# Summing modulation products over partitions: the data as the stationary operand, two columns of ones moving

## The reference

```
for l in range(2):
    m  = (silu(c)     @ w_mod[l] + b_mod[l])   # 9 x 1024, w_mod[l] is 1024 x 9216
    mc = (silu(c_ctx) @ w_mod[l] + b_mod[l])   # the same weights, other vector
    x  = ffn_sublayer(x,  m,  0, ...)          # x + 0.5*m[2] * swiglu(norm(x)*g*(1+m[1]) + m[0])
    xc = ffn_sublayer(xc, mc, 0, ...)
    x, xc = mixers with m[3..5]                # convolution, pooling, attention
    xc = ffn_sublayer(xc, mc, 2, ...)          # not in the last layer
    x  = ffn_sublayer(x,  m,  2, ...)          # m[6..8]
...
mod = silu(c_2) @ w_ada + b_ada                # 6 x 1024, for the second block
```

## Time and profile before

| | |
|---|---|
| median of 3 runs | 3150.01 us (3148.82 to 3151.47) |
| profiled execution, its own time | 3150.01 us |
| span of the profiled execution | 3148.2 us |
| TensorE busy | 2897.5 us (92%) |
| VectorE busy | 2185.4 us (69%) |
| ScalarE busy | 1230.0 us (39%) |
| GpSimd busy | 416.9 us (13%) |
| mean granted TensorE clock | 0.934 of full speed |
| first feed-forward stage, layer 0 | about 65 to 445 us |
| second feed-forward stage, layer 0 | about 705 to 1089 us |
| first feed-forward stage, layer 1 | about 1103 to 1471 us |

### The profile page before, as it was taken

The page is one execution under the profiler, slowest core; times in us unless marked ns, Lnnn a source line. Parts: engine busy times, 40 slices in busy tenths (PEclk is TensorE's granted clock), DMA queues, the critical chain, the costliest instruction groups (busy, mean ns, idle before and its releaser), DMA issues. The chain is left out here.

```text
span 3148.2 us, 45698 instructions
## 1 busy us (share of the span) xinstructions
PE 2897.5 (92%) x15462; PEld 2438.5 (77%) x15462; DVE 2185.4 (69%) x4149; ACT 1230.0 (39%) x2288; POOL 416.9 (13%) x455
## 2 busy tenths in 40 slices
PE   7999989999999999998989987697379999999998
PEld 4888868567888788887859986567268999999997
DVE  2999993549898875657466664355998777777775
ACT  2323233443222332223455453154125444444444
POOL 0111135011111200103300000000374000000000
PEclk9999989999999999998999998688559999999999
DMA  5455533133555544544415546014002566656563
GB/s 229 174 184 191 176 130 100 35 107 134 194 177 198 181 145 141 194 129 139 129 59 165 183 156 213 1 32 143 0 0 69 186 187 187 187 186 186 187 187 118
DMA packets 107701, 449.91 MB, mean 143 GB/s; under 512 B 11952, under 2 KB 12592, under 8 KB 94256
## 3 DMA queue, kind: packets, MB, share of 16 engines
q1 hardware_dynamic: 93744, 347.46, 34.7%
q0 software_dynamic: 13824, 100.67, 8.5%
HBM read 447.04 MB, written 1.05 MB: 142 GB/s over the span
## 5 line engine op out<-in xcount | busy, mean ns | idle before, releaser
L178 DVE TENSOR_TENSOR weight_lo<-weight_ring,weight_hi 128x512 fp32r<-128x512 f32 x1272 | 947.0, 747 | 561.7 <-ACT weight_hi L171 547.4
L171 ACT ACTIVATE weight_hi<-weight_ring 128x512 fp32r<-128x512 f32 x1272 | 797.9, 630 | 1162.3 <-PE bank L257 1160.8
L255 PE MATMUL bank<-operand_hi,weight_hi 128*128 128x256 f32 (+1 forms) x3168 | 1045.5, 330 | 43.0 <-DVE operand_lo L579 35.7
L256 PE MATMUL bank<-operand_lo,weight_hi 128*128 128x256 f32 (+1 forms) x3168 | 1042.4, 329 | 0.0
L257 PE MATMUL bank<-operand_hi,weight_lo 128*128 128x256 f32 (+1 forms) x3168 | 1041.9, 329 | 0.0
L255 PEld LDWEIGHTS bank<-operand_hi,weight_hi 128*128 128x128 f32 x3168 | 610.5, 193 | 107.3 <-issue 34.1
L256 PEld LDWEIGHTS bank<-operand_lo,weight_hi 128*128 128x128 f32 x3168 | 611.1, 193 | 55.7
L257 PEld LDWEIGHTS bank<-operand_hi,weight_lo 128*128 128x128 f32 x3168 | 610.4, 193 | 51.6
L813 DVE SCALAR_TENSOR_TENSOR extension_ffn<-extension_ffn,silu_c 128x512 f32<-128x512 f32 x532 | 388.4, 779 | 1.7
L255 PE MATMUL bank<-hidden_hi_ffn,weight_hi 128*128 128x512 f32 (+1 forms) x704 | 256.4, 364 | 4.2 <-DVE arena L1055 4.2
L256 PE MATMUL bank<-hidden_lo_ffn,weight_hi 128*128 128x512 f32 (+1 forms) x704 | 255.3, 363 | 0.0
(11 more groups left out here) (250 smaller groups left out, 2836.6 us busy)
## 6 DMA issues: line engine op xcount, KB each, us to landing
weight_ring<-in_ffn SPq DMA_DIRECT2D x272, 512.0 KB, 3.6
weight_ring<-in_experts SPq DMA_DIRECT2D x256, 512.0 KB, 3.5
extension_ffn<-in_w_mods POOLq DMA_DIRECT2D x96, 1024.0 KB, 7.5
weight_ring<-in_w_mix SPq DMA_DIRECT2D x56, 512.0 KB, 3.6
weight_ring<-in_w_second SPq DMA_DIRECT2D x52, 512.0 KB, 3.7
extension_mixer<-in_rel_bias SPq DMA_DIRECT2D x2, 1536.0 KB, 6.8
arena<-in_x SPq DMA_DIRECT2D x1, 2048.0 KB, 9.4
arena<-in_cmp_k SPq DMA_DIRECT2D x1, 2048.0 KB, 11.8
```

The source lines that it names most:

```text
L171: nc.scalar.activation(self.hi[:, g % 2, h], self.ring[:, g % NS, h], ACT.Copy).then_inc(self.rounded, 1)
L178: self.nc.vector.tensor_tensor(self.lo[:, g % 2, h], self.ring[:, g % NS, h], self.hi[:, g % 2, h].bitcast(F32), ALU.subtract).then_inc(se ...
L255: nc.tensor.matmul(out, a_hi, b_hi, start=start and n == 0, stop=False)
L256: nc.tensor.matmul(out, a_hi, b_lo, start=False, stop=False)
```

## The change

The sum over partitions swaps its operands. For each block of 128 features the tile's 128 x 128 block itself (`hi`, then `lo`) is the stationary operand, and two columns of ones move. The result then lies with features on the partitions, in two equal columns of PSUM, where `mod_sums` wants it. So `move` and `turn` go, with their signals, and `pick` is replaced by `ones_r` (128 x 2). `collect` reads every other column. Its place on VectorE's list, with the `finish` behind it, is now ahead of the addition of the last output chunk; it was after the stage's last chunk.

```
 def sum(self, pe, d):
         pe.wait_ge(self.halved.sem, self.halved.at(d + 1))
+        for n in range(self.blocks):                     # 4 * groups
+            at = 2 * self.blocks * d + 2 * n
+            out = c.bank[6 + (d < self.early)][:, at:at + 2]
+            b = slice(n * P, (n + 1) * P)
+            nc.tensor.matmul(out, self.hi[:, b], c.ones_r[:, :], start=True, stop=False)
+            last = nc.tensor.matmul(out, self.lo[:, b], c.ones_r[:, :], start=False, stop=True)
+        last.then_inc(self.summed.sem, 1)
-        for g in range(self.groups):
-            row = self.groups * d + g
-            pick = self.pick[:, ROWS - 1 - row:2 * ROWS - 1 - row]
-            out = c.bank[6 + (d < self.early)][0:ROWS, :]
-            nc.tensor.matmul(out, pick, self.hi[:, g * 512:(g + 1) * 512], ...)
-            last = nc.tensor.matmul(out, pick, self.lo[:, g * 512:(g + 1) * 512], ...)
-        last.then_inc(self.summed.sem, 1)
-    def move(self, act, upto): ...
-    def turn(self, pe, upto): ...
 def collect(self, dve, lo, hi):
-        dve.wait_ge(self.turned.sem, ...)
+        dve.wait_ge(self.summed.sem, self.summed.at(hi))
 Ffn.tensor:
-            if self.gate_first and n0 == 0:
-                work.turn(pe, work.early)
...
-        if work:
-            work.turn(pe, work.n)
 Ffn.scalar:
-                if self.gate_first and n0 == 0 and u == 13:
-                    work.move(act, work.early)
...
-                if work and n0 + nh == FT and n == KT - 1:
-                    work.move(act, work.n)
 Ffn.vector:
             for n in range(KT):
                 units.subtract(dve, 0, u0 + 2 * nh + n + 2, [0])
+                if work and n0 + nh == FT and n == KT - 1:
+                    work.collect(dve, KT // 4 if self.gate_first else 0, work.n)
+                    self.finish(dve)
                 dve.wait_ge(units.used, units.used_at(u0 + 2 * nh + n))
...
-        if work:
-            work.collect(dve, KT // 4 if self.gate_first else 0, work.n)
-            self.finish(dve)
 Start.gpsimd:
-        in_order(pool, chip.pool_step, nc.gpsimd.memset(self.pick[:, :].bitcast(F32), 0.0))
-        nc.gpsimd.memset(self.pick[:, ROWS - 1:ROWS].bitcast(F32), 1.0)
+        nc.gpsimd.memset(chip.ones_r[:, :].bitcast(F32), 1.0)
```

More of the change, by code:

```diff
@@ L35 @@
 LAYER_UNITS = N_MOD * KT // 2
-ROWS = 32
 MOD_UNITS = LAYERS * LAYER_UNITS + 6 * KT // 2
@@ L303, in __init__ @@
         self.eps = sb("eps", [P, 1])
+        self.ones_r = sb("ones_r", [P, 2], F32R)
         self.squared, self.summed, self.rooted = sig("squared"), sig("summed"), sig("rooted")
@@ L645, in __init__ @@
         self.chip, self.norm = chip, norm
-        self.stream, self.units, self.pick = stream, Units(stream, 0), chip.extra["pick"]
+        self.stream, self.units = stream, Units(stream, 0)
         self.n, self.slots = FIRST_UNITS, 4
@@ L755, in __init__ @@
         self.stepped = chip.mod_step.take(self.steps * self.n)
-        self.pick, self.rows = chip.extra["pick"], chip.part(A_RSTD, 512)[0:ROWS]
-        self.moved, self.turned = (s.take(1 + (early > 0)) for s in (chip.mod_moved, chip.mod_turned))
         self.rounded, self.halved, self.summed = (s.take(self.n) for s in (chip.mod_rounded, chip.mod_split, chip.mod_summed))
@@ L835, in sum @@
-        last.then_inc(self.summed.sem, 1)
[L837 to L850, removed]
+        for n in range(self.blocks):
[4 more added lines that the diff above has]
+            last = nc.tensor.matmul(out, self.lo[:, b], c.ones_r[:, :], start=False, stop=True)
@@ L852, in collect @@
+        last.then_inc(self.summed.sem, 1)
     def collect(self, dve, lo, hi):
         c, nc = self.chip, self.chip.nc
-        dve.wait_ge(self.turned.sem, self.turned.at(1 if hi == self.early or not self.early else 2))
+        dve.wait_ge(self.summed.sem, self.summed.at(hi))
         for g in range(self.groups):
-            src = c.bank[6 + (hi == self.early)][:, 0:4 * ROWS].rearrange("p (u b d g) -> p g d u b", u=2, b=2, g=self.groups)
+            src = c.bank[6 + (lo < self.early)][:, 2 * self.blocks * lo:2 * self.blocks * hi].rearrange("p (d g u b x) -> p d g u b x",
+                                                                                    g=self.groups, u=2, b=2, x=2)[:, :, g, :, :, 0]
@@ L858, in collect @@
             dst = c.mod_sums[:, self.first + 2 * lo:self.first + 2 * hi, 2 * g:2 * g + 2]\
                 .rearrange("p (d u) b -> p d u b", u=2)
-            last = nc.vector.tensor_copy(dst, src[:, g, lo:hi])
+            last = nc.vector.tensor_copy(dst, src)
         in_order(dve, c.dve_step, last)
@@ L1048, in vector @@
             if self.gate_first and n0 == 0:
-                work.collect(dve, 0, work.early)
+                work.collect(dve, 0, KT // 4)
                 finish_mod(chip, dve, 0, 2, 3)
@@ L2278, in build @@
             chip.take(first, T2, A_WORDS)
-            chip.take_more(first, "pooling", pool_w=([P, 2, P], F32), pool_inv=([P, 2, S], F32),
-                           pick=([P, 2 * ROWS - 1], F32R))
+            chip.take_more(first, "pooling", pool_w=([P, 2, P], F32), pool_inv=([P, 2, S], F32))
             x, h = chip.part(A_X, KT, T2), chip.part(A_H, KT, T2)
```

4 lines of the change are left out of this document (removed).

## The result

The changed kernel takes 3181.69 us, median of 4 runs (3179.18 to 3182.88); the kernel before took 3149.41 us beside it (4 runs, 3148.11 to 3151.47). The ratio is 1.0100, 95% interval 1.0086 to 1.0115: 32 us slower, where +30.8 us and 3180.8 us were forecast.

The account below looks back on a forecast made before the run. TensorE's instruction stream was taken to pace the feed-forward stages. Sums +29.6, turning -0.45, collect +1.05 and +0.6 us gave +30.8 on 3150.0, so 3180.8 us, with 3168 to 3198 for 8 in 10.

Parts of the forecast that it names:

- The pitch: In the sums on TensorE: narrow matmuls start 0.1135 us apart, not below about 0.103, the time of the 128-column load.
- right neighbour: L532's 128x128 stationary, two-column fp32 matmuls stand for the new sums: loads bound them, fixed 86 ns plus 0.8 ns a column.
- The burst: Each unit pair's sum on TensorE: 16 narrow matmuls cost +0.89 us with two groups, 8 cost +0.45 with one.
- How many count: Sums that lengthen the feed-forward stages: 13.6 of 16 in each two-group stage, the rest absorbed; all 12 in layer 1.
- The turning: Removing move and turn: the early one in the dense stretch saves 0.45 us, the other three 0.
- The end of the first stage: Layer 0's first feed-forward: collect and finish ahead of the last add, and a later last chunk, cost +0.6 us.
- cover of 0.64 us: First stage's end: time from the last square's end (447.02) to its L532 half's start (447.66), hiding part of collect and finish.
- The collect in the other stages: Collect and finish ahead of the last add: +1.05 us in layer 1's stage, 0 in the second, with 3.2 us of cover.
- The clock: Rival, 6%: narrow bursts let TensorE's clock fall, 2.7 us per climb back; 3287 us if every counted burst, 3207 if one in four.
- Loads exposed at 0.25 us: Rival, 5%: loads are not pulled ahead of such short matmuls on TensorE; pitch 0.25 us, 3254 us.
- The quick load: Rival, 3%: an fp32r load of 128 columns costs no more than 32; pitch 0.0325 us, 3138 us, a gain.
- VectorE hides the sums: Rival, 3%: TensorE truly follows VectorE, whose slack takes the added sum time; only +1.2 us stays, 3151 us.

## Why the prediction was right

**The pitch** (forecast 0.1135, measured 0.111). The argument that L532's bursts are the right neighbour, because the load bounds them, is what the runs tested hardest: 0.06 us for half the columns loaded, no change for 64 times the columns moved, 0.025 us with the short bf16 load, 0.11 us per matmul by the kernel with half of them. The load record of 64 columns lasts 138 ns, halfway between the 88 ns of 2 and the 191 of 128: the 0.8 ns a column of the prediction.

**The burst** (forecast +0.89 and +0.45, measured +0.90 and +0.45, from one burst to the next: 23.59 us against 22.69, and 22.70 against 22.25).

**How many count** (13.6 of 16 forecast). By the lag of each burst 14 count in full in both two-group stages. That of d = 14 is absorbed in both, as forecast; the last one is absorbed in the second stage alone.

**The turning** (-0.45 forecast): the lag grows by 0.35 us over it and not by 0.90, so -0.55.

**The end of the first stage** (+0.6 forecast). Up to the last burst's start the stage gained 11.5 us, where 13.6 x 0.89 - 0.45 = 11.65 was forecast. Behind it came +2.4: the last burst +0.86, the last chunk +1.7 by the clock, and from the last wide matmul to the spread -0.2. The prediction's cover of 0.64 us was made by TensorE's wait for GpSimd. This wait, 1.53 us before the change, was used up by the later chunk, so collect and finish lay bare (1.0 us by the kernel with the collect put back). The two nearly cancel in that last piece.

**The collect in the other stages.** Layer 1: +1.05 forecast, 1.08 measured up to the add, 1.3 up to the spread, as the norm's last sums then fell partly into the lower clock level (1.39 us for eight records instead of 1.05). Second stage: 0 forecast, and nothing is seen of it (-0.5 behind d = 14).

**The clock.** 6% was given to a fall after narrow bursts. It took place at large only when the bursts were twice as long. In the changed kernel it took place once, at the end of the first stage. That the last burst of this stage is the one with a wait ahead of it was written down in the prediction, and not put together with the clock; but a wait with a burst behind it did not bring the fall in every kernel, so its cause stays open.

**The start of layer 1's stage.** The stage gained 5.7 us: 12 x 0.45 = 5.4 by the sums, 1.4 at the end, and -1.1 ahead of its first burst. The two stretches of 14 us behind the milestone, before and after, differ in the granted clock:

```profile
1098.00:1112.00 14.00, 11.09 (x36) 9.03 (x37) 11.69 (x30) 6.71 (x16) 0.00 (x0) 0.62 0.07 28
```

```profile
1124.50:1138.50 14.00, 11.09 (x41) 9.14 (x42) 11.71 (x30) 6.73 (x16) 0.00 (x0) 0.70 0.08 32
```

0.08 of 14 us is the 1.1 us. The prediction had no term for this; why the clock was back earlier is open.

**The sum.** The bursts and the turn were forecast at 29.15 us and came to 12.0 + 12.6 + 5.4 = 30.0. The ends and starts of the three stages were forecast at 1.65 and came to 1.9 - 0.9 + 0.3 = 1.3, by other parts than the forecast ones: a fall of the clock in one stage and an earlier return in another nearly cancel. The stretches without any edit gave 0.6 + 0.3 - 1.3 = -0.4, less than what they differ by between executions (the start alone by up to 2.7 us over the kernels here). So the narrow matmuls, nearly all of the sum, came out by the prediction's own working, and that the ends did too is partly luck.

**The rivals.** Loads exposed at 0.25 us: the records do last 0.25, and the starts say 0.111. The quick load: real, but not for fp32r. VectorE hides the sums: only that of d = 14 in each two-group stage.

## What to carry to other kernels

Making the data the stationary operand and moving two columns of ones saves no TensorE time where the load of 128 columns takes 0.11 us and a matmul of 512 columns 0.23: count weight loads, not moving columns, and take a sum over partitions as narrow matmuls only if there are fewer than two of them for each wide one, or if their loads are short. Read the cost of an instruction from the distance between starts of its nearest relative, and ask what bounds that relative. Do not queue small work ahead of the last add of a stage when the next norm hangs on it, and when a tile's size changes, look at what moved behind it.

## What the runs showed of the hardware

- A weight load of 128 columns in fp32r lasts 191 ns and paces narrow matmuls at 0.111 us; in bf16 96 ns and 0.025 us. 64 columns in fp32r: 138 ns, 0.06 us.
- Spread among wide matmuls, a narrow one still costs 0.115 us, although a wide one takes 0.23 us and a load 0.11: only the load of the next matmul was hidden.
- Between fp32r and bf16 matmuls of 512 columns the load was not pulled ahead: 0.1 us or more at each change, 7 us for the whole kernel when only the types of the wide sum were changed. With two-column matmuls the starts show no such cost.
- Tiles shifted by some 126 bytes made fp32r matmuls of 512 columns stand 0.232 us apart instead of 0.227, some 9 us in all. Which tile's place it is was not tried.
- A TensorE without idle time can be granted less than the upper level: 0.95 in 80 to 440 us with bursts of 3.6 us of two-column matmuls between wide ones, also 0.95 where half of them moved 128 columns, and 1.00 with bursts of 1.8 us. After 0.67 us of waiting and a burst of 1.8 us, seven wide matmuls ran at 0.43 us each in two kernels; after 0.81 us and the same burst in a third kernel the clock stayed at 1.00.
